# A two-part network on one Trainium2 core: the seven products of each fast matrix product in another order, and all low halves of the gated branch on VectorE

## The reference

```python
def recurrent_block(h, w_x, w_y, conv_w, conv_b, w_a, b_a, w_i, b_i, lam_param, w_o):
    gate_branch = jax.nn.gelu(h @ w_y)
    xb = causal_depthwise_conv(h @ w_x, conv_w, conv_b)
    r = sigmoid(blockdiag(xb, w_a) + b_a); i = sigmoid(blockdiag(xb, w_i) + b_i)
    log_a = -RG_C * r * softplus(-lam_param); a = exp(log_a)
    u = sqrt(-expm1(2.0 * log_a)) * (i * xb)
    hs = associative_scan(a * hs + u)
    return (hs * gate_branch) @ w_o

def sqrelu_mlp(h, w1, w2):                       # w1: 1024 x 4096, w2: 4096 x 1024
    return jnp.square(jax.nn.relu(h @ w1)) @ w2

x = x + sqrelu_mlp(rmsnorm(x, mlp_norm_g[layer]), w1[layer], w2[layer])
```

## Time and profile before

| what | value |
|---|---|
| runs | 3583.86, 3578.41, 3581.73 us; median 3581.73 |
| the profiled execution | 3583.34 us, its span 3581.2 us, mean granted TensorE clock 0.979 |
| PE / PEld busy | 3399.5 us (95%) / 2668.2 us (75%) |
| DVE / ACT / POOL busy | 2466.7 us (69%) / 1558.7 us (44%) / 757.0 us (21%) |
| MLP 1, recurrent layer, MLP 2 | TensorE's first matmul at 651.52, 1274.24, 1600.01; behind its last matmul, keep_busy begins at 2223.67 |

### The profile page before, as it was taken

How to read it: one execution, slowest core, us unless ns; L and a number is a source line. 1 busy time by engine, 2 the same in 40 slices (tenths; PEclk the granted TensorE clock), 3 DMA queues, 4 the chain that set the end, 5 groups by cost and what they waited for, 6 DMA issues and landing times. The chain is left out here.

```text
span 3581.2 us, 43257 instructions
## 1 busy us (share of the span) xinstructions
PE 3399.5 (95%) x17006; PEld 2668.2 (75%) x17006; DVE 2466.7 (69%) x2845; ACT 1558.7 (44%) x2241; POOL 757.0 (21%) x439
## 2 busy tenths in 40 slices
PE   7999999999999989999999998899989989998898
PEld 6777777878778778787878787887646778764567
DVE  4666765898888989649887989476546442374666
ACT  2355453545454436425454454116345320443551
POOL 2455551000000037420000000232211222230214
PEclk9999999999999999999999999899999999999999
DMA  4234341221111121211111210231042121202413
GB/s 168 90 127 150 112 165 70 70 67 47 48 48 47 59 89 47 96 64 47 47 48 60 68 62 1 88 124 51 21 135 60 65 106 47 74 33 65 126 69 112
DMA packets 100595, 275.27 MB, mean 77 GB/s; under 512 B 9872, under 2 KB 11824, under 8 KB 100400
## 3 DMA queue, kind: packets, MB, share of 16 engines
q1 hardware_dynamic: 77104, 206.52, 17.5%
q10 hardware_dynamic: 16384, 40.90, 3.5%
q0 software_dynamic: 6912, 25.17, 2.1%
HBM read 220.39 MB, written 47.97 MB: 75 GB/s over the span
## 5 line engine op out<-in xcount | busy, mean ns | idle before, releaser
L933 PE MATMUL tk_aux<-tk_t,tk_s_hi 128*128 128x512 f32 x2048 | 512.9, 391 | 13.8 <-ACT tk_aux L1061 7.3
L1038 ACT CAST tk_s_hi<-tk_w 128x1024 fp32r<-128x1024 f32 x224 | 235.5, 1052 | 521.0 <-PE tk_aux L933 292.5
L933 PEld LDWEIGHTS tk_aux<-tk_t,tk_s_hi 128*128 128x128 f32 x2048 | 381.3, 188 | 106.6 <-issue 19.4
L933 PE MATMUL tk_acc<-tk_t,tk_s_hi 128*128 128x512 f32 x1536 | 380.2, 390 | 0.0
L1259 DVE TENSOR_TENSOR held_lo<-tk_w,tk_s_hi 128x1024 fp32r<-128x1024 f32 x224 | 273.7, 1222 | 107.4 <-ACT tk_s_hi L1038 107.2
L933 PEld LDWEIGHTS tk_acc<-tk_t,tk_s_hi 128*128 128x128 f32 x1536 | 288.3, 188 | 60.7 <-issue 1.0
L933 PE MATMUL tk_aux<-tk_t,held_lo 128*128 128x512 f32 x1024 | 274.0, 389 | 0.0
L933 PEld LDWEIGHTS tk_aux<-tk_t,held_lo 128*128 128x128 f32 x1024 | 192.2, 188 | 40.5
L175 POOL TENSOR_TENSOR pj_w_lo<-pj_w_raw,pj_w_hi 128x1024 fp32r<-128x1024 f32 x24 | 61.8, 2578 | 702.0 <-ACT pj_w_hi L150 700.4
L933 PE MATMUL tk_acc<-tk_t,held_lo 128*128 128x512 f32 x768 | 205.3, 389 | 0.0
L841 POOL CAST held_hi<-held_raw 128x1024 fp32r<-128x1024 f32 (+1 forms) x30 | 41.5, 1384 | 710.2 <-DVE tk_t L1275 596.9
(11 more groups left out here) (474 smaller groups left out, 8196.2 us busy)
## 6 DMA issues: line engine op xcount, KB each, us to landing
tk_w<-in_w_trunk SPq DMA_DIRECT2D x128, 512.0 KB, 4.1
da_w_mod<-in_ada_w POOLq DMA_DIRECT2D x48, 512.0 KB, 4.0
pj_w_raw<-in_w_in SPq DMA_DIRECT2D x44, 512.0 KB, 3.3
held_raw<-in_w_trunk SPq DMA_DIRECT2D x26, 512.0 KB, 3.3
held_raw<-in_w_qkv SPq DMA_DIRECT2D x24, 512.0 KB, 4.2
ma_w_raw<-in_w_out SPq DMA_DIRECT2D x24, 512.0 KB, 3.3
x_dram<-xT ACTq DMA_DIRECT2D x16, 512.0 KB, 4.4
xT<-x_dram SPq DMA_DIRECT2D x16, 512.0 KB, 7.0
```

What stands on the lines that cost most here:

```text
L933: last = pe.matmul(bank, w[:, d % 2, at:at + P], tr[:, f % 2, y, k, :], start=(j in (M1, M4, M5) and k == 0 and part == 0), stop=(k == 3 a ...
L1038: act.copy(tiles(s_hi[:, d % 2, :]), left(d)).then_inc(sems["s_hi"], 1)
```

## The change

Five edits, which belong together:

1. The order of the seven products becomes M1, M2, M4, M5, M6, M7, M3. The takes of M7 come one product earlier, those of M3 last; `relu_tile` comes before `relu_block`; the sum t3 (for M7) is made at d = 8, 9 instead of 10, 11; the DMAs for the next phase's weights are issued in another order.
2. In ScalarE's walk the copies of M1 (`take`) come ahead of `t_high`, and the squares move to the places where their relu is now due. In VectorE's down phase t1, t2 and t4 are made in another order around d = 1, 2.
3. Since M7 now finishes tiles 4 to 7 first, all steps into the recurrent layer and out of MLP 2 go by `TILES = [4, 5, 6, 7, 0, 1, 2, 3]`, and some adds of squares move ahead of the last two low halves.
4. `total(1, 0)` moves from the last chunk of panel R_X to the sixth chunk of panel R_X + 1, and panel R_X + 2 is made in a spare bank (`aux[:, 1, :]`), so that it waits for no read.
5. GpSimd's `y_low` is gone; VectorE makes all eight.

```diff
-    M1, M2, M4, M5, M6, M3, M7 = range(7)
+    M1, M2, M4, M5, M6, M7, M3 = range(7)
...
     def first_of_branch(k):
-        if k == DK - 1:
-            total(1, 0)
-        pe.wait_ge(sems["x_lo"], k + 1)
+        pe.wait_ge(sems["x_lo"], (k + 4) % DK + 1)
+
+    def second_of_branch(k):
+        if k == TILES[5]:
+            total(1, 0)
...
     pe.wait_ge(sems["read_dve"], wg.d_at[7, M7, 1])
-    linear(R_X, first_of_branch, 1)
-    pe.wait_ge(sems["read_dve"], wg.d_at[7, M7, 3])
-    linear(R_X + 1, None, 3)
+    pn.product(pe, 0, R_X // 2, *A, first_of_branch, TILES)
+    pe.wait_ge(sems["read_dve"], wg.d_at[7, M3, 3])
+    pn.product(pe, 1, R_X // 2, *A, second_of_branch, TILES)
+    pn.product(pe, 0, R_X // 2 + 1, *A, bank=aux[:, 1, :], spare=True)
+    linear(R_X + 3, None, 1)
+    evacuated(pe, R_X + 2)
...
 # ScalarE, mlp
     s_high(at + 1)
-    if ph % 2 and d < 2:
-        for p in (2 * d, 2 * d + 1):
-            square_tile(ph - 1, p)
-    if f + 1 < 56 * m + 56:
-        t_high(f + 1, d % 2)
+    if ph % 2 and d == 2:
+        for p in (2, 3):
+            square_block(ph - 1, 1, p)
...
     for p in (2 * q, 2 * q + 1):
         take(ph, jj, p)
+    if f + 1 < 56 * m + 56:
+        t_high(f + 1, d % 2)
...
 # VectorE, up
-    if d in (12, 13):
-        for p in (2 * d - 24, 2 * d - 23):
-            relu_block(ph, p)
+    if d == 13:
+        for p in (0, 1):
+            relu_tile(ph, p)
...
-    elif d in (10, 11):
+    elif d in (8, 9):
         t3_sum(ph, h)
...
 # VectorE, down
     if d == 1:
+        for p in (2, 3):
+            relu_block(ph - 1, p)
+    elif d == 2:
         t1_sum(ph, 1)
-    elif d in (2, 3):
+        t2_sum(ph, h)
+        t4_sum(ph, h)
+    elif d == 3:
         t4_sum(ph, h)
...
-    for kind, n in (((low, 0), (low, 1)), ((low, 2), (low, 3)), ((low, 4), (low, 5)),
-                    ((low, 6), (low, 7)) + tuple((partial(add_hidden_square, 1), n) for n in range(DK)))[step]:
+    for kind, n in (((low, 4), (low, 5)), ((low, 6), (low, 7), (square, 4), (square, 5)),
+                    ((low, 0), (low, 1), (square, 6)), ((low, 2), (low, 3), (square, 7), (square, 0),
+                                                        (square, 1), (square, 2), (square, 3)))[step]:
...
 # GpSimd
-    10: [(branch_low, 6), (branch_low, 7), (block_weights, 7), (y_low, 0)],
-    11: [(y_low, 1)], 12: [(y_low, 2)]}
+    10: [(branch_low, 6), (branch_low, 7), (block_weights, 7)]}
...
 # VectorE, recurrent layer
     if c is not None:
         branch(c)
+    if n > Y_BEHIND:
+        y_low(n - Y_BEHIND - 1)
     if n >= Y_BEHIND:
         gate(n - Y_BEHIND)
```

More of the change, by code:

```diff
@@ L197, in credit, with product @@
             pe.sem_inc(self.sems[f"panel_done{u}"], 1)
-    def product(self, pe, u, turn, h_hi, h_lo, before_chunk=None, order=None, behind=None):
+    def product(self, pe, u, turn, h_hi, h_lo, before_chunk=None, order=None, behind=None, bank=None, spare=False):
         pe.wait_ge(self.sems[f"w_split{u}"], turn + 2)
-        pe.wait_ge(self.sems[f"psum_free{u}"], turn + 1)
+        if not spare:
+            pe.wait_ge(self.sems[f"psum_free{u}"], turn + 1)
         order = order or ([c.k for c in self.prep.chunks] if self.prep else list(range(self.kc)))
+        bank = self.acc[:, u, :] if bank is None else bank
         for k in order:
@@ L208, in product @@
                 for s in range(2):
-                    last = pe.matmul(self.acc[:, u, s * HALF:(s + 1) * HALF], w[:, u, k, :],
+                    last = pe.matmul(bank[:, s * HALF:(s + 1) * HALF], w[:, u, k, :],
                                      h[:, k, s * HALF:(s + 1) * HALF],
@@ L705, in trunk @@
         wg = Winograd()
-        M1, M2, M4, M5, M6, M3, M7 = range(7)
+        TILES = [4, 5, 6, 7, 0, 1, 2, 3]
+        M1, M2, M4, M5, M6, M7, M3 = range(7)
         X_AHEAD, Y_BEHIND = 3, 5
@@ L1097, in mlp @@
                                 if ph % 2 == 0 and d == 13:
-                                    for p in range(4):
-                                        square_block(ph, 1, p)
+                                    for p in (0, 1):
+                                        square_tile(ph, p)
+                                if ph % 2 and d == 0:
+                                    for p in (2, 3):
+                                        square_tile(ph - 1, p)
+                                if ph % 2 and d == 1:
+                                    for p in (0, 1):
+                                        square_block(ph - 1, 1, p)
                                 if ph % 8 == 7 and d >= 12:
@@ L1194, in last @@
                     def last(step):
-                        for n in ((0, 1), (2, 3), range(4, DK))[step]:
+                        for n in ((4, 5), (6, 7), range(4))[step]:
                             final(1, n)
```

87 lines of the change are left out of this document (39 added, 48 removed).

## The result

The changed kernel takes 3589.73 us (median of nine executions, 3587.6 to 3595.08) against 3581.73 us for the kernel before. The ratio is 1.0026, with a 95% interval of 1.0016 to 1.0036: slower by 0.26%, where I had forecast 0.1% faster. The profiled execution is 3587.6 us, its span 3585.3.

The account below looks back on a forecast made before the run. It read TensorE's chain of waits as the bound, the largest sum in reach being 2.68 us in each of eight phase pairs. Terms -0.8 + 0.9 + 0.5 - 5.0 = -4.4 us from 3583.34 gave 3578.9; predicted 3578, range 3568 to 3584.

Parts of the forecast that it names:

- The pairs of phases: Up-to-down boundaries in the MLPs: stall moves from M2 to M4, -0.1 us per pair, -0.8 us in all.
- the new wait of 0.6 us: VectorE at the up-to-down boundary: s_high of M2's second half must wait until M1 is complete, 0.6 us.
- The sign of being wrong: MLP pairs of phases shorter than 154.5 us or longer than 155.6 would show the forecast wrong.
- My upper bound of +1.2 per pair: Pairs of phases: +1.2 us each if VectorE loses one more round trip to ScalarE of 1.17 us.
- Rival 3: Boundary: ScalarE comes two operations (2.1 us) later, each pair loses 1.9 us more, 15.2 in all, 3593 us; chance 0.08.
- Rival 2: Boundary stalls go for good: VectorE finds 2 us or more per pair, 3562 to 3572 us (3558 at the end); chance 0.24.
- The start of each MLP: First up phase: t_high of M4 now stands behind root and copies, +0.9 us in MLP 2, +0.5 in MLP 1.
- Into the recurrent layer: R_X to R_X + 3: 1.8 us stall in R_X, 9.5 us wait at R_X + 2 on GpSimd's weights, +0.6 us overall.
- The gated branch: R_Y + 5 starts 3.5 us earlier and 1.5 us of clock cost goes: -5.0 us, the entry's +0.6 included.
- The end of MLP 2: VectorE's work is the same in another order; the 10.9 us wait for the last squares stays: 0.

Follow-up runs that it names:

- e2: Changed kernel with two VectorE swaps per up-to-down boundary: t2's second half ahead of M4's first t_low, s_low behind the second t4; 3560.11 us, ratio 0.9939.
- e1: Changed kernel with TensorE repeating the first matmul of M4's first unit eight times more in each down phase; 3579.39 us, ratio 0.9993 to the kernel before.
- e6: Changed kernel with VectorE making all low halves ahead of all adds of squares into the recurrent layer; 3588.05 us, ratio 1.0016 to the kernel before.
- e3: Kernel before with only the gated branch's low halves moved from GpSimd to VectorE; 3575.71 us, ratio 0.9984.
- e4: Changed kernel with GpSimd splitting R_X + 2's weights ahead of the ai blocks and the reciprocal ahead of the softplus operations; 3585.51 us, ratio 1.0011.
- e5: Changed kernel with TensorE making the six matmuls on t's first half first in M4's first unit in each down phase; 3572.65 us, ratio 0.9973.
- e10: Changed kernel with the edits of e2 and e6 alone; 3561.98 us, ratio 0.9938 to the kernel before.

## Why the prediction was wrong

I forecast 3578 us and "no change"; it came out at 3590. Point by point:

- **The pairs of phases: the step that failed.** The count of VectorE's work held: the second t4 comes within 0.2 us of where I put it, and the new wait of 0.6 us came as 0.56. "I take -0.1 us per pair, -0.8 us" rests on "the loss moves from M2 to M4: 2.5 to 2.6 us where it was 2.68". Place, releaser and length of the stall were right (2.19 us at M4, 2.85 with what follows, so +0.15 where I had -0.1), and e2 shows that VectorE's row was the cause. But I counted the loss as a length only, as if one stall of 2.2 us cost what several of up to 0.75 cost. The loss of clock behind it stands in my sum at nothing, without a reason. It came in six pairs of eight, 1.2 to 1.6 us each, 9.1 in all, and e1 shows that it is the clock: with the same wait and work in front of it, the 9.1 us are gone. The sign of being wrong that I had named, pairs longer than 155.6 us, stands in the profile: 156.4 to 156.8 where the clock fell. I had the warning at hand: the earlier trace rows price the clock behind a long stall, and I used it for the recurrent layer alone. My upper bound of +1.2 per pair was another round trip on VectorE, not this.
- **The rivals.** None was it. Rival 3 has the right side and, with 3593 us, nearly the time, but by luck: ScalarE was not late, it stood idle until VectorE had made t4. Rival 2 was one edit away: e2 is its case, and its 3560 us lie between the 3558 and the 3572 that I gave for it.
- **Not counted:** the memset in the last phase, +0.84.
- **The start of each MLP.** +0.9 and +0.5 forecast. The first up phases lose 4.38 us in MLP 2 and 2.97 in MLP 1, where they lost 3.53 and 2.62: +0.85 and +0.35.
- **Into the recurrent layer, the second term that was mis-sized.** The wait at R_X + 2 came as forecast, 8.76 us on GpSimd's low half (9.5). The stalls in R_X are 3.49 us, not 1.8. I had priced the adds ahead of the low halves at 3.9 us for three and left out that GpSimd's split of R_X + 1 would fall on two of them. So the root is 23.8 us behind R_X's start instead of 23.0, where I had 21.6. e6 shows that these adds are the cause: without them ahead, the root is at 21.7. How much of it is the collision is read from the rows only.
- **The gated branch.** -3.5 to R_Y + 5 and -1.5 behind it: e3, with the old entry, measures -3.2 and -1.4. In the changed kernel it is -1.0 and -1.4, since the entry took back 2.2; with the entry mended (e6) R_Y + 5 comes 3.9 us earlier than before.
- **The end of MLP 2.** Forecast 0; -1.1 us, 0.9 of it in the wait for the last squares (10.0 us where it was 10.9).

With the clock added to my sum of -4.4 (9.1), the memset (0.8), the pairs' 0.25 x 8 and the late entry (2.6), less 1.1 at the end of MLP 2 and 0.2 at the starts, it gives +8.8, where the stages show +8.7. One slip of arithmetic: 3578.9 less 1.6 is 3577.3, not the 3578 that I wrote; nothing hangs on it.

## What to carry to other kernels

Price a stall on TensorE by its length and by what it does to the clock: here 2.85 us in one piece cost up to 4.5 where 2.7 in pieces cost 2.7. When a wait moves, read who ends it and whether that engine itself stands idle for a round trip; work put into that idle time (two swaps here) did more than the whole reordering. And two edits that each gain must be looked at together when one puts GpSimd's SBUF work beside VectorE's.

## What was not expected of the hardware

- A stall of 2.19 us was followed by the lower clock in 19 of 24 cases (three profiles of kernels that keep this stall: the change, e4, e6), one of 2.40 us in panel R_X in three of five profiles (e1, e2, e5, but not the change and e4), one of 1.28 us in none of eight (e5), one of 1.51 us at the start of MLP 2 in three of nine profiles (e1, e6, e10). What decides a case was not settled; the first pair of MLP 2 kept its clock in all three profiles with the 2.19 us stall.
- Matmuls whose result is thrown away kept the clock up, and the pair of phases took no longer for them: with 1.8 us of them it lost 2.84 to 2.87 us, and 2.85 without them in the two pairs of the changed kernel that kept the clock.
- Eight adds with both inputs in SBUF took 10.53 us alone and 13.19 beside a GpSimd cast and subtraction (1.32 and 3.26 us; the subtraction takes 2.39 beside a reciprocal, which has one input). Both engines lost time.
